# Alternating a pair's two heads in TensorE's queue, behind one mask product per bank, in the last mixer's attention

## The reference

```
logits = q @ k.T * scale                       # 256 queries x 256 keys, 64 channels
p = softmax(where(key <= query, logits, -1e30))
o_sel = p_sel @ v_sel ; o_win = p_win @ v_win  # two branches: "selected" keys and "window" keys
o_cmp = p_cmp @ v_cmp                          # 15 compressed keys
out = gate0 * o_cmp + gate1 * o_sel + gate2 * o_win
```

## Time and profile before

| | |
|---|---|
| time, median of 3 runs | 1838.37 us (1838.35 to 1844.88) |
| span of the profiled execution, first to last instruction | 1828.2 us |
| the profiled execution's own time | not given apart from its span |
| TensorE (PE) busy | 1783.9 us, 98% of the span |
| VectorE (DVE), ScalarE (ACT) busy | 51%, 44% |
| mean granted TensorE clock | 0.981 of full speed |
| chain that ended last | PE 92% of it |
| attention of the last mixer in the span | 1494.9 to 1605.8 us |

### The profile page before, as it was taken

How to read it: one execution, slowest core, us unless ns; L and a number is a source line. 1 busy time by engine, 2 the same in 40 slices (tenths; PEclk the granted TensorE clock), 3 DMA queues, 4 the chain that set the end, 5 groups by cost and what they waited for, 6 DMA issues and landing times.

```text
span 1828.2 us, 30525 instructions
## 1 busy us (share of the span) xinstructions
PE 1783.9 (98%) x12700; PEld 1636.3 (90%) x12721; DVE 939.8 (51%) x934; ACT 805.1 (44%) x875; POOL 67.6 (4%) x76
## 2 busy tenths in 40 slices
PE   8989999999899999999999999999999999999999
PEld 7988899989789998999898999999999866689998
DVE  5484545454454545445565544455544844334444
ACT  5413555443455544344434334454334434335552
POOL 0031000000000001000000000000000300000000
PEclk9998999999999999999999999999999979799999
DMA  8552465575255555555554555565555450025562
GB/s 278 164 111 95 152 201 175 173 230 184 70 166 190 184 168 183 186 190 178 172 198 150 184 184 184 184 187 197 179 193 168 129 162 1 1 74 184 182 203 93
DMA packets 237472, 296.40 MB, mean 162 GB/s; under 512 B 7147, under 2 KB 217279, under 8 KB 237408
## 3 DMA queue, kind: packets, MB, share of 16 engines
q1 hardware_dynamic: 231128, 284.39, 47.2%
q10 hardware_dynamic: 6280, 11.09, 2.6%
HBM read 291.27 MB, written 3.15 MB: 161 GB/s over the span
## 4 chain that ended last, share of the span: by engine, by line
PE 92%; DVE 3%; DMA 2%; ACT 1%; issue 1%; POOL 1%; SPq 0%; ACTq 0%; POOLq 0%; DVEq 0%
PE ps L1515 20%; PE ps L1425 18%; PE ps L1429 17%; PE ps L1426 17%; PE ps L1452 3%; PE ps L1456 3%; PE ps L1453 3%; DMA raw<-in_hgrn_w_out 2%; PE ps L1637 1%; PE ps L1648 1%; PE ps L1472 1%; PE ps L1462 1%; PE ps L1633 1%; PE ps L1760 1%; PE ps L1827 1%
## 5 line engine op out<-in xcount | busy, mean ns | idle before, releaser
L916 DVE TENSOR_TENSOR wlo<-raw,whi 128x2048 fp32r<-128x2048 f32 x265 | 607.3, 2295 | 550.1 <-ACT whi L514 549.6
L1425 PE MATMUL ps<-xhi,whi 128*128 128x256 f32 x2656 | 653.2, 284 | 4.2 <-ACT xhi L546 1.8
L1426 PE MATMUL ps<-xhi,wlo 128*128 128x256 f32 x2656 | 651.5, 283 | 0.0
L514 ACT ACTIVATE whi<-raw 128x2048 fp32r<-128x2048 f32 x265 | 505.4, 1908 | 327.7 <-PE ps L1429 182.1
L1425 PEld LDWEIGHTS ps<-xhi,whi 128*128 128x128 f32 x2656 | 509.2, 192 | 9.4 <-issue 6.5
L1426 PEld LDWEIGHTS ps<-xhi,wlo 128*128 128x128 f32 x2656 | 509.6, 192 | 2.3
L1429 PE MATMUL ps<-xlo,whi 128*128 128x256 f32 x2656 | 372.8, 283 | 0.0
L1429 PEld LDWEIGHTS ps<-xlo,whi 128*128 128x128 f32 x2656 | 342.7, 192 | 0.0
L1515 PE MATMUL ps<-whi,hhi 128*128 128x512 f32 x480 | 187.5, 391 | 0.0
L1515 PE MATMUL ps<-wlo,hhi 128*128 128x512 f32 x480 | 187.5, 391 | 0.0
L1515 PE MATMUL ps<-whi,hlo 128*128 128x512 f32 x480 | 186.7, 389 | 0.0
(11 more groups left out here) (213 smaller groups left out, 1428.6 us busy)
## 6 DMA issues: line engine op xcount, KB each, us to landing
raw<-in_ffn_w_gate_up SPq DMA_DIRECT2D x88, 1024.0 KB, 5.1
raw<-in_ffn_w SPq DMA_DIRECT2D x66, 1024.0 KB, 5.0
raw<-in_ffn_w_down SPq DMA_DIRECT2D x44, 1024.0 KB, 4.9
raw<-in_hgrn_w_in SPq DMA_DIRECT2D x16, 1024.0 KB, 5.4
raw<-in_moba_w_in SPq DMA_DIRECT2D x12, 1024.0 KB, 5.1
raw<-in_conv_w_in SPq DMA_DIRECT2D x12, 1024.0 KB, 5.2
raw<-in_kv_w SPq DMA_DIRECT2D x6, 1024.0 KB, 5.1
raw<-in_hgrn_w_out SPq DMA_DIRECT2D x4, 1024.0 KB, 17.2
```

Of the source, the lines that this page charges most:

```text
L514: act.activation(whi[c % RING][:, 0:width], raw[c % RING][:, 0:width], ACT.Copy).then_inc(split_hi, 1)
L916: dve.tensor_tensor(wlo[c % RING][:, 0:width], raw[c % RING][:, 0:width], whi[c % RING][:, 0:width].bitcast(F32), ALU.subtract).then_inc(s ...
L1425: pe.matmul(out, hi[:, k, tile], xhi[:, k, :], start=k == 0, stop=False)
L1426: pe.matmul(out, lo[:, k, tile], xhi[:, k, :], start=False, stop=False)
```

## The change

In `logits` the mask is now written first, by one product of 384 columns for each of the two banks; the scores of the two heads are then added on top in alternation: first tile of head 0, first tile of head 1, second tile of head 0, second tile of head 1. In `pv` the products of the two heads alternate as well, the compressed keys of both heads first. `mask_b` grows from 256 to 384 columns to hold the mask of a whole bank, and VectorE fills it once near the start. No other engine's program changes. In `moba` the score products of the two heads alternate too.

```diff
-        mask_b = sb("mask_b", [P, 2 * P], BF16)
+        mask_b = sb("mask_b", [P, 3 * P], BF16)
...
-                    dve.tensor_copy(mask_b[:], causal[:, P:3 * P]).then_inc(zero_ready, 1)
+                    dve.tensor_copy(mask_b[:], causal).then_inc(zero_ready, 1)
...
                 def logits(u):
                     if u >= 2:
                         pe.wait_ge(exp_ready if masked else max_ready, at.att + u - 1)
-                    for a in range(2):
-                        q, k = q_of(u, a), k_of(u, a)
-                        bank = 2 * (u % 2) + a
-                        mm = pe.matmul(ps[:, bank, 0:P], q[:, 0:P], k[:, 0:P], start=True, stop=not masked)
-                        if masked:
-
-                            mm = pe.matmul(ps[:, bank, 0:P], ident_b[:], mask_b[:, P:2 * P], start=False, stop=True)
-                        mm = pe.matmul(ps[:, bank, P:3 * P], q[:, P:S], k, start=True, stop=not masked)
-                        if masked:
-                            mm = pe.matmul(ps[:, bank, P:3 * P], ident_b[:], mask_b[:], start=False, stop=True)
+                    first_bank = 2 * (u % 2)
+                    if masked:
+                        for a in range(2):
+                            pe.matmul(ps[:, first_bank + a, 0:3 * P], ident_b[:], mask_b[:], start=True, stop=False,
+                                      skip_group_check=True)
+                    for part, tile, keys in ((slice(0, P), slice(0, P), slice(0, P)), (slice(P, 3 * P), slice(P, S), slice(0, S))):
+                        for a in range(2):
+                            mm = pe.matmul(ps[:, first_bank + a, part], q_of(u, a)[:, tile], k_of(u, a)[:, keys],
+                                           start=not masked, stop=not masked or part.stop == 3 * P, skip_group_check=masked)
                     mm.then_inc(scored, 1)
...
                 def pv(u, pt):
                     pair, branch = u // 2, u % 2
                     g = pair // 2
-                    for a in range(2):
-                        hd = 2 * pair + a
-                        out = [ps[a * HD:(a + 1) * HD, 6 + t, 0:P] for t in range(TT)]
-                        if branch == 0:
-                            rows_c = slice(32 * (hd % 4), 32 * (hd % 4) + N_CMP)
-                            for t in range(TT):
-                                pe.matmul(out[t], vc[rows_c, g, :], cpt[rows_c, g, t * P:(t + 1) * P], start=True, stop=False)
-                        v = vn[:, branch, :, g * HD:(g + 1) * HD]
-                        last = branch == 1
-                        pe.matmul(out[0], v[:, 0, :], pt[:, a, 0:P], start=False, stop=last)
-                        pe.matmul(out[1], v[:, 0, :], pt[:, a, P:2 * P], start=False, stop=False)
-                        mm = pe.matmul(out[1], v[:, 1, :], pt[:, a, 2 * P:3 * P], start=False, stop=last)
+                    heads = [(a, ps[a * HD:(a + 1) * HD, 6:8, 0:P]) for a in range(2)]
+                    if branch == 0:
+                        for t in range(TT):
+                            for a, out in heads:
+                                rows_c = slice(32 * ((2 * pair + a) % 4), 32 * ((2 * pair + a) % 4) + N_CMP)
+                                pe.matmul(out[:, t, :], vc[rows_c, g, :], cpt[rows_c, g, t * P:(t + 1) * P], start=True, stop=False)
+                    v = vn[:, branch, :, g * HD:(g + 1) * HD]
+                    last = branch == 1
+                    for t, keys, part in ((0, 0, 0), (1, 0, 1), (1, 1, 2)):
+                        for a, out in heads:
+                            mm = pe.matmul(out[:, t, :], v[:, keys, :], pt[:, a, part * P:(part + 1) * P], start=False,
+                                           stop=last and part != 1)
                     return mm
```

## The result

| | before | after |
|---|---|---|
| median | 1838.36 us (1817.34 to 1844.88, 4 runs) | 1775.84 us (1775.23 to 1776.32, 4 runs) |
| span of the profiled execution | 1828.2 us | 1773.4 us |
| attention of the last mixer | 1494.94 to 1605.82, 110.9 us | 1494.34 to 1551.89, 57.6 us |

What follows compares the result with a forecast made beforehand. TensorE was taken to bound the last mixer's attention. Gains of 21.6 (scores with masks), 10.6 and 1.4 (values) and 5.9 (clock), less 0.4 at the end, sum to 39.1 us: 1838.4 to 1799.3 us, range 1788 to 1815.

Steps and rivals of the forecast that it cites:

- What lies around it, 10.2 us, stays.: Outside the profiled span: the 10.2 us between the span of 1828.2 and the time of 1838.4 us stays unchanged.
- The clock term: Last mixer's attention: the clock costs the same share as now, 10.9 us instead of 16.8, so 5.9 us gained.
- the clock rival: Last mixer's attention: the clock sinks to half for the whole stage, 1836 us, no change; chance 0.07.
- The scores, 1.06 us: Scores of a unit in `logits`: 1.06 us if weight loads queue up; with masks 1.49 instead of 2.84, 21.6 us gained.
- The values: Value products in `pv`: branch 0 takes 1.43 instead of 2.75 us, branch 1 0.89 instead of 1.07; 10.6 and 1.4 gained.
- TensorE stays the bound with 0.3 us to spare.: Attention stage after the change: TensorE needs 3.45 us a unit, the longest loop through the engines 3.1.
- The loop that I worked out, 6.25 us: Attention stage: turn, copy, exponentials, scores and values up to the turn two units later, 6.25 us for two units.
- much shorter than 1.27: Scores in the attention stage: only if they were much shorter than 1.27 us would TensorE begin to wait.
- the serial compressed keys: Branch-0 values: two heads' compressed keys can't write one bank at once, 3.4 us comes back, 1802.7 us; chance 0.17.
- switches between heads cost a passage: Scores and values: every switch of partitions or columns costs 0.17 to 0.2 us, +13.3 us, 1852 us; chance 0.06.
- The rival that partitions never overlap: Scores and values: products on different partitions never run side by side, only passages are saved, 1811 us; chance 0.20.

Runs made afterwards that it cites:

- the kernel before with fillers: The kernel before with two more 512-column filler products behind the values of each of 14 units; 1823.64 us, ratio 0.9954.
- the values alone: The kernel before with only `pv` changed, so the two heads alternate in the values, `logits` as it was; 1805.61 us, ratio 0.9853.
- the scores alone: The kernel before with only `logits` changed, masks first and scores in alternation, `pv` as it was; 1787.48 us, ratio 0.9748.
- the mask per head: The changed kernel with each head's mask product right ahead of its own two score products; 1787.01 us, ratio 0.9743.
- scores by head: The changed kernel with both score products of head 0 before those of head 1, behind the two masks; 1774.67 us, ratio 0.9677.

## Why the prediction was wrong

The direction and the mechanism were right: passages between shapes saved, heads side by side, no time given back behind the stage. The size was wrong, in two terms that concern the same thing, the clock, and in smaller ones.

1. **"What lies around it, 10.2 us, stays."** This step failed. In every run whose span is on record, the time is 1.7 to 1.9 us above it, before and after (1844.64 against 1842.9, 1775.23 against 1773.4). The 10.2 us, and with it the sentence on them under the profile before, came from setting the span of one execution against the median of others. The profiled execution itself took about 1828.2 + 1.8 = 1830.0 us, with a mean clock of 0.981; executions near the median show 0.976. So 8.4 us of the median's loss to the clock had been put down to something that no kernel can change, and it went away. By the spans the gain is 54.8 us, by the medians 62.5.

2. **The clock term.** I let it cost 10.9 us afterwards, the same share as before. This step failed as well, and it is the largest term: it costs nothing, for the stage is at 1.00 throughout, so the whole 16.8 us came back instead of 5.9. (That 16.8 was sized well: the clock was at 0.50 for 39.1 us of the stage before, which by the factor of 1.82 cost 17.6, an estimate.) The row that I used against the clock rival (the streaming share rises) should have moved the centre too. That the clock goes with how much streams is supported by the kernel before with fillers (mean clock of the stage 0.82 before and 0.95 with more work) and by the stages of the values alone (0.90), the scores alone (0.96) and the mask per head (1.00). It is not settled what exactly brings it down. Without these two terms, 19.3 us of the 23.5 that the forecast missed, it would have been 1780.0 us.

3. **The scores, 1.06 us.** Mis-sized: 0.86 measured, next to the 0.84 worked out for heads side by side without queued weight loads. The loads of two heads on different partitions don't queue up; 0.20 x 16 = 3.2 us.

4. **The values.** 1.43 and 0.89 were forecast, 1.38 and 0.80 measured; the lags do not appear, 1.1 us. The turn takes 0.71 us up to the mask product instead of the 0.80 up to scores: 16 x 0.09 = 1.4 us. Turn and mask product both have 128 partitions, so this is the passage into the scores, which I had not counted there.

5. **"TensorE stays the bound with 0.3 us to spare."** Wrong, though cheap. The loop that I worked out, 6.25 us, runs through scores and values. The one that binds runs through the other engines: behind the exponentials come the high and the low part of the pair, and the maxima of the next unit stand behind the low part in VectorE's queue. It takes 6.57 against TensorE's 2 x 1.28 + 1.38 + 0.80 + 2 x 0.71 = 6.16, so some 0.4 us a pair was lost to it, 2.4 us in six waits, which moving the step brought back. Waits were to begin only with a unit's scores "much shorter than 1.27"; they began at 1.28.

In spans: 39.1 forecast, + 10.9 clock, + 3.2 scores, + 1.1 + 1.4 values and turn, - 2.4 loop = 53.3, and 53.3 was measured in the stage. The remaining 1.5 us of the span lie outside it: 0.6 ahead, and 0.9 behind, where before the clock had stayed low for the first 1.9 us of the next stage.

Of the rivals, the serial compressed keys didn't come: two heads' products, on different partitions and columns, go to one bank in 0.58 us together, and in the trace after the records of the two heads start 0.01 us apart. The Trainium skill ("TensorEngine Tiling (Array Packing)", Restrictions and Gotchas) states that different row tiles can't access one PSUM bank at the same time. The trace doesn't agree for these two products, and no run here shows a cost of it. That switches between heads cost a passage is refuted by the same rows. The rival that partitions never overlap is refuted by the version with a mask per head.

How the 62.5 us divide: executions of the kernel before with a mean clock of 0.987 to 0.990 take 1816 to 1819 us, so about 21 us go with the clock. Of the other 41, work and waits make 36.5 by the terms above (53.3 - 16.8). The rest fits the clock that even those executions still lose: 0.989 against the 0.992 of the changed kernel is some 12 us more at half clock, about 5 us, an estimate by the factor of 1.82.

## What to carry to other kernels

Group TensorE's products by the partitions and columns that they use; a single product of another shape between them costs two passages (0.31 us together for a mask product between scores) and, worse, keeps small products on different parts of the array from running side by side. Where two products of the same operand can be made one, join them (0.61 us a unit here for the masks of the two heads). Alternating matters little beside that. Before taking a median minus a span as a constant, look whether the executions differ in clock, and when a change makes TensorE's stage denser, count the clock's part of the stage as gain too. And when the busiest engine gets lighter, write out the loop through the other engines with each one's queue order in it.

## What the runs showed of the hardware

- Eight float32 score records on two halves of the partitions take 0.86 us and four on one half take 0.85: the second half is free, weight loads included. The same holds for 15-partition products (0.58 for four and for eight).
- The heads run side by side without alternation: whole for scores of four records a head, with a lag of 0.28 us for values of six records a head (1.08 against 0.80). The two cases differ in more than the number of records (scores of the two heads lie on different partitions, values on the same ones with different columns), and no run tells which of the two makes the lag. "TensorE: Matmul & The Clock Gate" in the Trainium skill (Part 3, The mechanism) has matmuls start and end in strict program order; the earlier trace rows and the version with scores by head, where head 1 starts 0.01 us after head 0, disagree for the start.
- The granted clock fell to 0.50 for up to 13.5 us with TensorE never idle, and did so differently from one execution to the next; the kernel before spread over 1815.6 to 1849.5 us with mean clocks of 0.990 to 0.970, the changed one over 1772.2 to 1779.6 with 0.994 to 0.990.
